# Where buffers lie in SBUF: halves and stage memory at the low end, permanent buffers at the upper end

## The reference, cut to what matters

```python
def swiglu(h, w1, w3, w2):
    return (jax.nn.silu(h @ w1) * (h @ w3)) @ w2
...
        y = even_mixer(...)        # layer 0: x @ w_in, Fourier mix, window attention, @ w_out
        y = pool_mix(...)          # layer 1: moving averages, a product in four groups
        h = h + g1 * y
        h = h + g2 * swiglu(modulate(rms_norm(h, ...)), ffn_w1[layer], ffn_w3[layer], ffn_w2[layer])
...
        x = x + 0.5 * swiglu_2(rms_norm_2(x, ...), ffn1_wg, ffn1_wu, ffn1_wd)
        h = rms_norm_2(x, ...) @ w_in        # 2840 columns, for sparse and stick-breaking attention
        x = x + concatenate([o_nsa, o_sb]) @ w_out
        x = x + memory_cross_attention(...)
        x = x + 0.5 * swiglu_2(rms_norm_2(x, ...), ffn2_wg, ffn2_wu, ffn2_wd)
```

## The kernel before

| buffer | first byte | past a multiple of 512 |
|---|---|---|
| `xT`, `xh`, `xl` | 16,512; 32,896; 49,280 | 128 |
| `raw0`, `raw1` | 65,664; 73,856 | 128 |
| `wh0`, `wh1`, `wl0`, `wl1` | 82,048; 90,240; 98,432; 106,624 | 128 |
| `acc` | 114,816 | 128 |
| `tmp0` to `tmp3`, `ssum` | 127,680 and on | 192 |
| first byte of every stage | 138,208 | 480 |
| `mh`, `ml` | 138,208; 146,400 | 480 |
| `fb0` and on | 154,592 | 480 |
| `hh`, `hl` (each net) | 138,208; 183,264 | 480 |
| `oh`, `ol` | 158,688; 162,784 | 480 |

## Time and profile before

### The profile page before, as it was taken

The page is one execution under the profiler, slowest core; times in us unless marked ns, Lnnn a source line. Parts: engine busy times, 40 slices in busy tenths (PEclk is TensorE's granted clock), DMA queues, the critical chain, the costliest instruction groups (busy, mean ns, idle before and its releaser), DMA issues.

```text
span 2391.8 us, 24532 instructions
## 1 busy us (share of the span) xinstructions
PE 2253.5 (94%) x10300; PEld 1772.1 (74%) x10300; DVE 1099.2 (46%) x1550; ACT 775.8 (32%) x1149; POOL 87.6 (4%) x84
## 2 busy tenths in 40 slices
PE   6998999999994999999999999899998898999999
PEld 4666778888873888888888888677754576888887
DVE  3637765555428433333543323453474346443421
ACT  3314432222223322222322222322456735322211
POOL 0000000000001000000111100100000001111100
PEclk9999999999996999999999999899899998999999
DMA  7521145565520232323223223223100020323222
GB/s 258 187 88 60 55 140 194 178 199 177 179 95 18 94 100 90 100 97 96 93 89 105 87 97 99 67 87 117 36 1 1 0 81 26 106 89 105 87 94 84
DMA packets 190782, 236.56 MB, mean 99 GB/s; under 512 B 4096, under 2 KB 175392, under 8 KB 190544
## 3 DMA queue, kind: packets, MB, share of 16 engines
q1 hardware_dynamic: 189696, 230.42, 29.7%
q0 software_dynamic: 976, 4.57, 0.6%
HBM read 231.96 MB, written 2.10 MB: 98 GB/s over the span
## 4 chain that ended last, share of the span: by engine, by line
PE 84%; DVE 8%; ACT 5%; issue 2%; DMA 0%; POOL 0%; SPq 0%; DVEq 0%; ACTq 0%; POOLq 0%
PE ps L399 24%; PE ps L401 24%; PE ps L400 24%; PE ps L679 2%; ACT pr L608 2%; PE ps L992 1%; PE ps L842 1%; PE ps L579 1%; PE ps L465 1%; PE ps L646 1%; DVE pr L633 1%; PE ps L1973 1%; DVE wl L348 1%; PE ps L378 1%; DVE sa L1391 1%
## 5 line engine op out<-in xcount | busy, mean ns | idle before, releaser
L399 PE MATMUL ps<-xh,wh 128*128 128x512 f32 x1800 | 714.6, 397 | 48.6 <-DVE xl L688 27.3
L400 PE MATMUL ps<-xl,wh 128*128 128x512 f32 x1800 | 707.2, 393 | 0.0
L401 PE MATMUL ps<-xh,wl 128*128 128x512 f32 x1800 | 706.8, 393 | 0.0
L348 DVE TENSOR_TENSOR wl<-raw,wh 128x2048 fp32r<-128x2048 f32 (+1 forms) x170 | 379.1, 2230 | 496.3 <-ACT wh L336 496.3
L399 PEld LDWEIGHTS ps<-xh,wh 128*128 128x128 f32 x1800 | 341.7, 190 | 127.7 <-issue 25.3
L336 ACT CAST wh<-raw 128x2048 fp32r<-128x2048 f32 (+1 forms) x170 | 315.3, 1854 | 344.2 <-PE ps L401 272.2
L401 PEld LDWEIGHTS ps<-xh,wl 128*128 128x128 f32 x1800 | 341.3, 190 | 73.4
L400 PEld LDWEIGHTS ps<-xl,wh 128*128 128x128 f32 x1800 | 342.0, 190 | 71.9 <-issue 1.2
L401 PE MATMUL ps<-hh,wl 128*128 128x512 f32 x704 | 280.9, 399 | 0.0
L400 PE MATMUL ps<-hl,wh 128*128 128x512 f32 x704 | 277.4, 394 | 0.0
L399 PE MATMUL ps<-hh,wh 128*128 128x512 f32 x704 | 276.2, 392 | 0.0
(11 more groups left out here) (331 smaller groups left out, 1965.7 us busy)
## 6 DMA issues: line engine op xcount, KB each, us to landing
raw<-in_ffn_w SPq DMA_DIRECT2D x52, 1024.0 KB, 5.3
raw<-in_ada_w SPq DMA_DIRECT2D x42, 1024.0 KB, 5.3
raw<-in_ffn_wg SPq DMA_DIRECT2D x22, 1024.0 KB, 5.3
raw<-in_ffn_wu SPq DMA_DIRECT2D x22, 1024.0 KB, 5.3
raw<-in_ffn_w SPq DMA_DIRECT2D x16, 896.0 KB, 5.1
raw<-in_ffn_wd SPq DMA_DIRECT2D x16, 896.0 KB, 4.7
raw<-in_w_in SPq DMA_DIRECT2D x10, 1024.0 KB, 5.2
raw<-in_ffn_wd SPq DMA_DIRECT2D x8, 1024.0 KB, 5.1
```

Source lines behind the costliest of these rows:

```text
L348: e.tensor_tensor(wl[s][:, 0:n], r[:, 0:n], wh[s][:, 0:n].bitcast(F32), ALU.subtract).then_inc(*WLO.up(i))
L399: e.matmul(dst, ah, bh, start=start, stop=False)
L400: e.matmul(dst, ah, bl, start=False, stop=False)
L401: return e.matmul(dst, al, bh, start=False, stop=stop)
```

## The change

`xh` and `xl` stay on the left, at the low end, and come first there; the memory of the stages follows right above them. All other permanent buffers, from `xT` to `dum`, are taken from the right, the upper end, by a new function `sbr`. Sizes, order of the declarations, instructions and semaphores are the same.

```diff
--- before.py
+++ after.py
@@ -181,30 +181,33 @@
         def sb(name, shape, dt=F32, stack=ctx):
             return stack.enter_context(nc.sbuf_tensor(name, shape, dt))
 
+        def sbr(name, shape, dt=F32):
+            return ctx.enter_context(nc.sbuf_tensor(name, shape, dt, side="right"))
+
         ps = ctx.enter_context(nc.psum_tensor("ps", [P, 8 * 512], F32))
         pb = [ps[:, i * 512:(i + 1) * 512] for i in range(8)]
 
-        xT = sb("xT", [P, NC, T])
         xh = sb("xh", [P, NC, T], F32R)
         xl = sb("xl", [P, NC, T], F32R)
-        raw = [sb(f"raw{i}", [P, SLOT]) for i in range(2)]
-        wh = [sb(f"wh{i}", [P, SLOT], F32R) for i in range(2)]
-        wl = [sb(f"wl{i}", [P, SLOT], F32R) for i in range(2)]
-        acc = sb("acc", [P, 1024])
-        vec = sb("vec", [P, NVEC])
-        cst = sb("cst", [P, NCST])
-        bcs = sb("bcs", [P, NBCS], BF16)
-        ada = [sb("ada0", [P, 48]), sb("ada1", [P, 48])]
-        adac = sb("adac", [P, 16])
-        sc = sb("sc", [P, 8, 2])
-        cf = sb("cf", [P, 48])
-        kmT = sb("kmT", [P, 2, LC])
-        vm = sb("vm", [P, 2, LC])
-        tmp = [sb(f"tmp{i}", [P, 512]) for i in range(4)]
-        ssum = sb("ssum", [P, 512])
-        sm = sb("sm", [P, 2, 16])
-        hs = sb("hs", [P, 4, 8])
-        dum = sb("dum", [P, 1])
+        xT = sbr("xT", [P, NC, T])
+        raw = [sbr(f"raw{i}", [P, SLOT]) for i in range(2)]
+        wh = [sbr(f"wh{i}", [P, SLOT], F32R) for i in range(2)]
+        wl = [sbr(f"wl{i}", [P, SLOT], F32R) for i in range(2)]
+        acc = sbr("acc", [P, 1024])
+        vec = sbr("vec", [P, NVEC])
+        cst = sbr("cst", [P, NCST])
+        bcs = sbr("bcs", [P, NBCS], BF16)
+        ada = [sbr("ada0", [P, 48]), sbr("ada1", [P, 48])]
+        adac = sbr("adac", [P, 16])
+        sc = sbr("sc", [P, 8, 2])
+        cf = sbr("cf", [P, 48])
+        kmT = sbr("kmT", [P, 2, LC])
+        vm = sbr("vm", [P, 2, LC])
+        tmp = [sbr(f"tmp{i}", [P, 512]) for i in range(4)]
+        ssum = sbr("ssum", [P, 512])
+        sm = sbr("sm", [P, 2, 16])
+        hs = sbr("hs", [P, 4, 8])
+        dum = sbr("dum", [P, 1])
 
 
         first = ExitStack()
```

## The result

The changed kernel takes 2432.64 us, median of 4 runs (2427.89 to 2436.03), against 2395.89 us (2392.07 to 2400.25, 4 runs) for the kernel before: a ratio of 1.0147, with a 95% interval of [1.0131, 1.0162]. The change makes it 1.5% slower, by 36.8 us. The profiled execution has a span of 2430.4 us where it was 2391.8, at the same mean granted clock of 0.966.

The account below looks back on a forecast made before the run. The prediction took TensorE, busy for 94% of the span and mostly in `mm3`'s matmuls, as the bound. +29 us for `xh`, -2 for `hh` and `oh` and -2 for weight waits gave 2395.56 + 25 = 2421 us, range 2380 to 2434.

Parts of the forecast that it names:

- The direction and its mechanism: Split matmuls of `mm3`: only addresses change, matmul time follows them, and the kernel gets slower, +25 us; chance of slower 0.65.
- Address phases, read from the earlier trace: Matmuls in `mm3`: 226.7 ns streaming `xh` at 128, 233.4 ns streaming `hh` at 480, so time follows addresses.
- The new pair at 232.5 ns: 512-column matmuls with moving side at 128, weights at 480: cost 232.5 ns, as without a lock between the streams.
- a poor lock: Matmuls streaming `hh` in the kernel before: they too fall into a lock between the two streams, at 233.4 ns.
- The term of `xh`: Matmuls streaming `xh`: 5000 of 5400 go from 226.7 to 232.5 ns, +29 us, all on the path.
- the term of `hh` and `oh`: The 2160 matmuls streaming `hh` or `oh`: from 233.4 to 232.5 ns each, -2 us.
- 2 us absorbed by less waiting for weights: TensorE's 5.8 us of waits for weights: slower matmuls give weights more time to arrive, -2 us.
- Rival 4: All 512-column matmuls run at `hh`'s 233.4 ns: 2430 us; counted within the forecast's own range, together 0.66.
- All else at nothing: Plain fp32 matmuls, VectorE, ScalarE and loads of `raw` add nothing; the 256-column matmuls 1 us either way.
- Rival 1: Placement doesn't matter, `hh` and `oh` are slower for a reason of their own: 2395.6 us; chance 0.11.
- Rival 2: Only the moving side's address counts, so `hh` and `oh` get 226.7 ns: -14.5 us, 2381 us; chance 0.16.
- Rival 3: The new pair is quicker, as with 256 columns, 224.4 ns per matmul: -31 us, 2364 us; chance 0.07.

Follow-up runs that it names:

- e1: The changed kernel with 352 unused bytes ahead of `xT` at the upper end, so all distances become 0: 2385.14 us, ratio 0.9946 to the kernel before.
- e6: The changed kernel with 352 unused bytes below `xh`, so moving and stationary operands are all at 480: 2381.41 us, ratio 0.9944 to the kernel before.
- e5: The kernel before with unused bytes between weight buffers and below stages, `hh`/`hl` read from 16 bytes in, giving distances 32, 224, 48, 240: 2423.37 us, one run.
- e2: The kernel before with 160 unused bytes below the first stage, so the stages start at 128 instead of 480: 2380.47 us, ratio 0.9931.
- e3: The changed kernel with 32 unused bytes ahead of `xT`, putting the weights at 448 and the distance at 320: 2425.02 us, one run.

## Why the prediction was right, and where its size was off

**The direction and its mechanism held.** Only addresses change; the distance between the streamed halves and the weights is what costs; `xh` loses its good distance, and `hh` gets the same as `xh`. e1 and e6 show it by taking the distance away again and leaving all of the change in place: ratios of 0.9946 and 0.9944 instead of 1.0147.

**Address phases, read from the earlier trace rows.** Right, with one refinement. The prediction spoke of weights that are "off", even or odd with 64. What the cost follows is the distance modulo 256 (in one case, 48 in e5, not that alone), and of the ten tried only 0 is good (226.7), 192 nearly.

**The new pair at 232.5 ns, "the unlocked cost".** This step failed in size. The prediction had noted that `hh` falls into "a poor lock", and then priced the new pair as if it fell into none. It falls into one of its own, at 234.3 ns, and is in it from the second matmul after a pause (350.73 to 356.12), so there is no "cost without a lock" to be seen in it. Nor does `xh` before begin slowly after every break: where it follows on other products of TensorE, the 22 steps from 1150.60 to 1155.59 take 4.99 us, 226.8 ns each, from the first on. The term of `xh` is then 5000 x (234.3 - 226.7) = +38 us, not +29, and the term of `hh` and `oh` 2160 x (234.3 - 233.4) = +2 us, not -2. The `hh` part of the second net shows the latter by itself, 123.4 - 122.9 = 0.5 us, and there are four such parts.

**2 us absorbed by less waiting for weights.** Wrong. The waits of TensorE after, for the same cause as the earlier trace rows:

```profile
PE ps L402 <- DVE wl L351: 6.0, 5, 2.4
```

They were 5.8 us and are 6.0; nothing is absorbed. Three of them, in the projections of the second block, make up 4.9 us before (1.42, 2.42 and 1.08, the first of them at 1600.92) and 4.9 after (1.41, 2.44 and 1.07). Inside the first net one grew from 0.30 to 0.80 us, and one of 0.41 us at 785.82 is gone. Why the three don't shrink beside slower matmuls was not tried.

Put together, 38 + 2 = +40 us against +38.6 in the span and +36.8 in the medians; predicted were +25. Rival 4, the poor lock for all, had priced it at 2430 us. That the range of 2380 to 2434 us holds the measured 2432.64 is narrow and in part luck: it lies 1.4 us inside the upper end, which was drawn for `xh` at 234 ns, and one of the four runs (2436.03) lies above it.

**All else at nothing.** Right. The kernel after: VectorE's groups by line and form, and the page's loads of one unit (columns as in the earlier trace rows).

```profile
L691 DVE TENSOR_TENSOR hl<-tmp,hh 128x512 fp32r<-128x512 f32 x88 | 60.9, 692 | 60.4 <-ACT hh L1248 60.4
...
L714 DVE TENSOR_TENSOR ssum<-ssum,tmp 128x512 f32<-128x512 f32 x35 | 24.1, 690 | 17.5 <-ACT tmp L707 17.5
...
raw<-in_ffn_w SPq DMA_DIRECT2D x52, 1024.0 KB, 5.4
```

692 and 690 ns where they were 693 and 690, though `hl` moved from 480 to 128 and `ssum` to the other end; 5.4 us for a load that took 5.3. In plain fp32, the timeline after, 41 to 75:

```profile
54.48 7.03 PE L845 MATMUL ps<-raw,scp 128*8 128x512 f32 x16
...
66.68 7.03 PE L845 MATMUL ps<-fb,scp 128*8 128x512 f32 x16
```

Again 7.03 us for 16, with `raw` now at 480 and `fb` at 128. The unit with the 608-byte pitch reads 22 steps in 5.12 us and in 5.08 us, to the hundredth what the earlier trace rows give: the rows of its weights go through many phases, so that moving them all changes little.

**The rivals.** Rival 1, that placement does not matter, gave 2395.6 us, and with it the rule of the Trainium skill, "SBUF — State Buffer", section "Who interferes with whom", that TensorE's two read ports are independent and that it never waits. The measurement decides against it, with 52 us between e2 (2380.47) and the changed kernel (2432.64). Rival 2, that only the moving side counts, falls with `xh`, whose moving side kept its phase and which lost 7.6 ns. e2 does land on this rival's 2381 us, but by making the pair equal, and not by where the moving side is. Rival 3, the new pair as better, came from 256-column matmuls. That row did not carry over: at 512 columns the same pair of phases is the slowest but one in the table. Nor is equal phase the best at 256 columns. In e3, where `wh` is streamed at 448 against `xh` at 128 (distance 192), a stretch reads, first and last of 95 starts:

```profile
1711.97 0.28 PE L404 MATMUL ps<-wl,xh 128*128 128x256 f32 x1
...
1722.62 0.28 PE L405 MATMUL ps<-wh,xl 128*128 128x256 f32 x1
```

10.65/94 = 113.3 ns, and the stretch before it, at the same distance, 11.19/95 = 117.8 (1699.65 to 1710.84), against 119.8 at distance 0.

**What stays open.** Why 0 and, nearly, 192 are good, in what the two streams meet, and what picks one of the two rhythms at 48, no run shows. Only multiples of 32 and two of 16 were tried. The table is for 512 columns alone, at a row pitch of 2048 bytes for the moving operand and 1024 for the weights, and other traffic was never taken away.

## What to carry to other kernels

Where TensorE is the bound in fp32r with 512 moving columns, give moving operand and weights the same phase modulo 256 bytes: 160 unused bytes below the stages make this kernel 0.7% faster than it was, and a regrouping of buffers that breaks the phase makes it 1.5% slower. A stack that hands out memory in steps of 32 bytes sets this phase unseen, and anything declared earlier can change it, so work out the addresses, and give the distance by a pad. Read it in the distance between starts over a hundred matmuls or more, at a stated clock; durations overlap, and a run at another shape (256 columns, plain fp32) or at the lower clock says nothing of it.

## What the runs showed of the hardware

- An fp32r matmul with 512 moving columns and 128 weight columns, at full clock and without a wait, costs from 226.7 to 234.6 ns, by the distance of its two operands' addresses modulo 256. Equal phase is good at 128 and at 480, with the weights in either end of the partition (226.7 in before, e1, e2 and e6).
- The dependence is no slope: 192 costs 228.9 ns and 240 costs 231.5, but 224 between them costs 233.6.
- Each pair settles into a rhythm of its own, and this need not be quicker than the beginning: at distance 0, 232.5 ns after one pause, then 226.7; at 352, 234.3 from the second matmul on. One distance can have two rhythms: 230.0 and 234.6 ns at 48 in e5.
- At granted clock 0.50 the same matmul costs 426 to 427 ns at distance 0 and at 352 alike.
- With 256 moving columns the distances rank otherwise: 119.8 ns at 0, and 113.3 and 117.8 in two stretches at 192 (e3).
- Plain fp32 matmuls (16 in 7.03 us before and after), VectorE's passes (693 and 692 ns), ScalarE (busy for 775.8 and 775.2 us) and the DMA's loads (5.3 and 5.4 us) show none of it.
